# Late spread, late squares, a halved first weight unit and dummy matmuls in a two-layer streaming encoder step

## The reference

```python
for i in range(DEPTH):                       # 2 layers
    hp, hs = rms_norm(xp, mix_norm_g[i]), rms_norm(xs, mix_norm_g[i])
    if i % 2 == 0:                           # layer 0: spatial gating
        # z = gelu(h @ w_in); u, v = split(z); v = rms_norm(v)
        # y = u * (ws @ v in blocks of 128 positions + b);  m = y @ w_out
        mp, ms = sgu_mixer(hp, ...), sgu_mixer(hs, ...)
    else:                                    # layer 1: latent attention, 16 heads
        # a = h @ w_in; c_q, c_kv, k_r = split(a), each rms-normed (k_r rotated)
        # q = c_q @ w_uq; k, v = c_kv @ w_ukv; softmax(q k) v; @ w_o
        # the samples also see 1024 cached latents
        ...
    xp, xs = xp + mp, xs + ms
    xp = xp + square(relu(rms_norm(xp, g) @ w_up[i])) @ w_down[i]    # width 4096
    xs = xs + square(relu(rms_norm(xs, g) @ w_up[i])) @ w_down[i]
```

## Time and profile before

| | us |
|---|---|
| median of 3 runs | 1505.07 |
| lowest and highest | 1504.78, 1507.0 |
| the profiled execution | 1505.77 |
| its span, first to last instruction | 1504.0 |
| PE busy in it | 1474.6 |
| DVE, ACT, POOL busy | 799.6, 629.3, 765.8 |

### The profile page before, as it was taken

The page is one execution under the profiler, slowest core; times in us unless marked ns, Lnnn a source line. Parts: engine busy times, 40 slices in busy tenths (PEclk is TensorE's granted clock), DMA queues, the critical chain, the costliest instruction groups (busy, mean ns, idle before and its releaser), DMA issues.

```text
span 1504.0 us, 29170 instructions
## 1 busy us (share of the span) xinstructions
PE 1474.6 (98%) x10552; PEld 1384.2 (92%) x10552; DVE 799.6 (53%) x1417; ACT 629.3 (42%) x1248; POOL 765.8 (51%) x517
## 2 busy tenths in 40 slices
PE   9999999999999999999999999999999999999998
PEld 7789999999999999999996767686999999999998
DVE  6005716755654636537856464655446636456365
ACT  4413200123434434335447575767225435344342
POOL 7454455453463453644776464847433544535534
PEclk9999999999999999999999999999999999999999
DMA  7222242222232131331433010101121241412312
GB/s 233 86 82 82 60 121 72 68 84 62 66 115 82 60 122 42 121 102 57 142 112 97 2 57 1 56 0 56 43 71 58 84 127 43 139 56 84 112 56 91
DMA packets 36384, 120.32 MB, mean 80 GB/s; under 512 B 6040, under 2 KB 6744, under 8 KB 36064
## 3 DMA queue, kind: packets, MB, share of 16 engines
q1 hardware_dynamic: 30240, 109.20, 23.4%
q10 hardware_dynamic: 6080, 10.28, 2.2%
HBM read 115.91 MB, written 3.55 MB: 79 GB/s over the span
## 4 chain that ended last, share of the span: by engine, by line
PE 48%; ACT 2%; DVE 1%; issue 1%; ACTq 0%; DVEq 0%
PE ps L673 8%; PE ps L675 8%; PE ps L674 8%; PE ps L809 5%; PE ps L811 5%; PE ps L810 5%; PE ps L1065 2%; PE ps L905 2%; PE ps L1015 1%; PE ps L1029 1%; PE ps L910 1%; PE ps L1018 1%; ACT kT L1897 1%; PE ps L994 1%; DVE lat L1437 1%
## 5 line engine op out<-in xcount | busy, mean ns | idle before, releaser
L673 PE MATMUL ps<-h_hi,w_hi 128*128 128x288 f32 x1280 | 380.6, 297 | 0.0
L674 PE MATMUL ps<-h_lo,w_hi 128*128 128x288 f32 x1280 | 377.6, 295 | 0.0
L675 PE MATMUL ps<-h_hi,w_lo 128*128 128x288 f32 x1280 | 376.3, 294 | 0.0
L604 POOL TENSOR_TENSOR w_lo<-raw,w_hi 128x512 fp32r<-128x512 f32 x128 | 173.4, 1364 | 220.3 <-ACT w_hi L1725 220.0
L809 PE MATMUL ps<-op_hi,w_hi 128*128 128x288 f32 x896 | 266.3, 297 | 4.3 <-DVE x L1351 4.2
L810 PE MATMUL ps<-op_lo,w_hi 128*128 128x288 f32 x896 | 265.0, 296 | 0.0
L811 PE MATMUL ps<-op_hi,w_lo 128*128 128x288 f32 x896 | 264.2, 295 | 0.0
L675 PEld LDWEIGHTS ps<-h_hi,w_lo 128*128 128x128 f32 x1280 | 241.1, 188 | 0.0
L673 PEld LDWEIGHTS ps<-h_hi,w_hi 128*128 128x128 f32 x1280 | 239.8, 187 | 1.2
L674 PEld LDWEIGHTS ps<-h_lo,w_hi 128*128 128x128 f32 x1280 | 240.3, 188 | 0.0
L595 POOL TENSOR_TENSOR w_lo<-raw,w_hi 128x1024 fp32r<-128x1024 f32 x60 | 145.3, 2426 | 183.9 <-ACT w_hi L1717 183.9
(11 more groups left out here) (195 smaller groups left out, 2777.9 us busy)
## 6 DMA issues: line engine op xcount, KB each, us to landing
raw<-stream SPq DMA_DIRECT2D x206, 512.0 KB, 3.6
out_x<-x ACTq DMA_DIRECT2D x8, 288.0 KB, 2.5
x<-xt SPq DMA_DIRECT2D x4, 288.0 KB, 5.9
x<-xt ACTq DMA_DIRECT2D x4, 288.0 KB, 8.9
raw<-stream ACTq DMA_DIRECT2D x2, 512.0 KB, 6.9
b_bc<-bs ACTq DMA_DIRECT2D x2, 512.0 KB, 6.1
cache_raw<-cache_ct ACTq DMA_DIRECT2D x1, 1024.0 KB, 5.6
v_out<-sgu_grow ACTq DMA_DIRECT2D x1, 512.0 KB, 5.0
```

Source lines behind the costliest of these rows:

```text
L604: nc.gpsimd.tensor_tensor(block_of(w_lo, b), factor(i, b), block_of(w_hi, b).bitcast(F32), ALU.subtract).then_inc(split_lo, 1)
L673: nc.tensor.matmul(out, l_hi, r_hi, start=first, stop=False)
L674: nc.tensor.matmul(out, l_hi, r_lo, start=False, stop=False)
L675: return nc.tensor.matmul(out, l_lo, r_hi, start=False, stop=last)
```

## The change

It has five parts.

- **First unit.** POOL splits unit 0 in two halves of 512 columns, with a semaphore `first_half`; PE computes all five tiles with the first half, then with the second. The dummies at the start are 25 in place of 16.
- **First spread.** `norm_spread(0)` moves from chunk 0 to behind unit 2 of chunk 3, into banks 3 and 4, and waits there for ACT's reads of chunk 2. PE's wait for `rms_bc_set` moves behind chunk 3; ACT's `norm_take(0)` moves ahead of the reads of chunk 3. ACT loads the Gelu table early.
- **Order of reads.** In chunks 0 to 2 ACT reads tiles 3 and 4 first, then 0 to 2 (`v_place` gives a tile's place).
- **Late squares.** In the last quarter of the first MLP the squares of blocks 4, 5 and 6 go to three places of their own (`late_sq`, over `v_out`), and DVE adds them, and that of block 7, at the very end (`add_last_squares`). `norm_sums(2)` moves one unit later in chunk 4.
- **Dummies.** Two steps ("warm", n) in `attention_order`, each three dummy matmuls of `ident`, ahead of the transpose of key tile 11 and ahead of the sample scores.

```diff
-    steps = [("key", KT_N - 3), ("score", 0), ("score", 1), ("key", KT_N - 2), ("score", 2), ("key", KT_N - 1),
+    steps = [("key", KT_N - 3), ("score", 0), ("score", 1), ("warm", KT_N - 2), ("key", KT_N - 2), ("score", 2), ("key", KT_N - 1),
+             ("warm", KT_N - 1),
              ("samples", 0)]
...
+        late_sq = place("late_sq", [P, 3, T], F32, bump[0] - 4 * 512 - 4 * DS)
...
-        WARM, WARM_BANK = 16, 2
+        KEY_FILL = (3, 3)
+        WARM, WARM_BANK = 25, 2
...
+        def spread_banks(n):
+
+            return (3, 4) if n == 0 else (5, 6)
+
+        def v_place(t):
+
+            return t - 3 if t >= 3 else t + 2
...
-            for u in range(SLOTS):
+            left, right = slice(0, UNIT // 2), slice(UNIT // 2, UNIT)
+            pool.wait_ge(raw_loaded[0], 16)
+            nc.gpsimd.tensor_scalar(w_hi[:, 0, left], raw[:, 0, left], 1.0, 0.0, ALU.mult, ALU.add).then_inc(first_half, 1)
+            pool.wait_ge(first_half, 1)
+            nc.gpsimd.tensor_tensor(w_lo[:, 0, left], raw[:, 0, left], w_hi[:, 0, left].bitcast(F32),
+                                    ALU.subtract).then_inc(first_half, 1)
+            nc.gpsimd.tensor_scalar(w_hi[:, 0, right], raw[:, 0, right], 1.0, 0.0, ALU.mult, ALU.add).then_inc(split_hi, 1)
+            pool.wait_ge(split_hi, 1)
+            nc.gpsimd.tensor_tensor(w_lo[:, 0, right], raw[:, 0, right], w_hi[:, 0, right].bitcast(F32),
+                                    ALU.subtract).then_inc(split_lo, 1)
+            for u in range(1, SLOTS):
                 split(u, u, 0, first=True)
...
-                for j in range(4):
+                for j in range(1 if h_count == 0 else 0, 4):
...
-                            pe.wait_ge(tok_read, chunk * 5 + t + (1 if t < 3 else 6))
+                            if chunk < 4:
+                                pe.wait_ge(tok_read, 5 * chunk + v_place(t) + (1 if t < 3 else 6))
+                            else:
+                                pe.wait_ge(tok_read, chunk * 5 + t + (1 if t < 3 else 6))
...
+            pe.wait_ge(first_half, 2)
+            for k in range(2):
+                if k:
+                    pe.wait_ge(split_lo, 1)
+                pe.wait_ge(h_ready, k + 1)
+                w = slice(k * 512, k * 512 + 512)
+                for t in range(NT):
+                    last = three(ps[0:ROWS[t], bank_of(0, t), 0:512], h_hi[:, k, cols(t)], h_lo[:, k, cols(t)],
+                                 w_hi[:, 0, w], w_lo[:, 0, w], k == 0, False)
+            last.then_inc(unit_done, 1)
             token_chunk(0, 0, 0, 512, h_count=0,
-                        between={2: lambda: norm_sums(0), 3: lambda: norm_spread(0)})
+                        between={2: lambda: norm_sums(0)})
             pe.wait_ge(var_set, 2)
+            pe.wait_ge(pair_set, 2)
+
+            def spread_first():
+                pe.wait_ge(tok_read, 10 + 15)
+                norm_spread(0)
+
+            for c in range(1, 4):
+                token_chunk(c, c % 2, 4 * c, 512, pack=True, between={2: spread_first} if c == 3 else None)
             pe.wait_ge(rms_bc_set, 2)
-            pe.wait_ge(pair_set, 2)
-            for c in range(1, 4):
-                token_chunk(c, c % 2, 4 * c, 512, pack=True)
...
-            token_chunk(4, 0, L_IN, QL, between={1: lambda: norm_sums(2)}, h_count=2 * KD, tiles=F_O, halves_apart=True)
+            token_chunk(4, 0, L_IN, QL, between={2: lambda: norm_sums(2)}, h_count=2 * KD, tiles=F_O, halves_apart=True)
...
+                def warm(j):
+
+                    pe.wait_ge(vals_set, g * KT_N + (KT_N - 2))
+                    for _ in range(KEY_FILL[j - (KT_N - 2)]):
+                        nc.tensor.matmul(ps[:, key_bank(KT_N - 4), 0:P], ident[:], ident[:], start=True, stop=True)
...
+            def add_last_squares(s):
+
+                dve.wait_ge(x_sq, 8 * s)
+                for n, sq in enumerate((late_sq[:, 0, :], late_sq[:, 1, :], late_sq[:, 2, :], act_t[:, 1, :])):
+                    dve.wait_ge(sq_added, 9 * s - 7 + PAIRS + n)
+                    nc.vector.tensor_tensor(sq_sum[:], sq_sum[:], sq, ALU.add).then_inc(sq_added, 1)
...
-                            next_operand(i + 3, 1, next_s, 2 * i - 1)
+                            low_part(i + 3, next_s, 2 * i - 1)
...
-                        next_operand(7, 1, next_s, 7)
+                        low_part(7, next_s, 7)
+                        add_last_squares(next_s)
...
-            norm_take(0)
-
-
             act.wait_ge(rms_set, 1)
+            nc.scalar.activation(junk[:, 1:2], rms_tok[:, 0:1], ACT.Gelu)
             act.wait_ge(set_up, SETUPS)
             for c in range(4):
                 parity = c % 2
-                for t in range(NT):
+                if c == 3:
+                    norm_take(0)
+                for t in (range(NT) if c == 3 else (3, 4, 0, 1, 2)):
...
-                            operand_and_square(i + 4, 1, next_s)
+                            act.wait_ge(stored, 16)
+                            operand_and_square(i + 4, 1, next_s, i if i + 1 < PAIRS else None)
```

29 lines of the change are left out of this document (19 added, 10 removed).

## The result

The changed kernel took 1493.08 us (median of six runs, 1492.78 to 1493.48), the kernel before 1505.03 us beside it (1504.67 to 1507.0). The ratio of the runs, compared round by round, is 0.9915, 95% interval 0.9905 to 0.9925; on 1505.07 us, the median of before at the time of the forecast, that is 1492.3 us, a gain of 12.8 us (11.3 to 14.3). (The two medians alone give 0.9921 and 1493.1 us.) So it is faster, as forecast, and by more than forecast: trace against trace the gain is 12.3 us (span 1504.0 to 1491.7), where the sum had 10.7. The changed kernel's own median lies 0.3 us inside the lower end of the range, the time by the ratio 0.5 us under it.

A forecast was written before the change was run, and what follows sets the result against it. PE's own work was taken as the bound (busy 1474.6 of 1504.0 us), so only holes, passes and low clock pay. 2.2 + 2.7 + 2.8 + 3.0 = 10.7 us off 1505.77 gave 1495.1 us, range 1492.8 to 1499.2.

The forecast's parts named there:

- tail term: Put-off square adds on DVE before the statistics, after the first MLP: 0.5 us lost at the latents' transposes, bounds 0 and -4.8.
- Part A: Start: halved first unit and more dummies let PE begin 0.45 us sooner at full clock (1.73 us), 2.2 us gained.
- Rival 3: Start: dummies hold the first unit, PE begins up to 1.8 us later than summed, 1497 us, chance 0.05.
- Part B: First spread: waits of 2.25 and 1.73 us go, moved passes cost 1.25 us in chunk 3, 2.7 us gained.
- the bank wait: PE's wait at the next chunk's fourth tile for ACT to read its bank, 1.73 us, claimed to vanish.
- Part C: Last quarter of first MLP: put-off squares gain 1.7 us idle and 1.6 us low clock, less 0.5: 2.8 us.
- The hole: PE's 2.44 us idle before DVE's add into x, last quarter of first MLP: to shrink by 1.7 us.
- the low clock: Half-speed stretch of 3.3 us after that idle time in the first MLP's last quarter: 1.6 us gained by avoiding it.
- rival 2: Put-off square adds at 2.96 us each hold the statistics up: 1499.4 us, 1501 with a clock fall, chance 0.10.
- Part D: Head groups: dummies in holes before last key and sample scores keep full clock, 3.0 us gained, bounds 0 and 3.0.
- Rival 1: Clock still falls somewhere, each fall costing 1.25 to 1.75 us: 1496.4 to 1498.5 us, chance 0.24.
- Rivals 4 and 5: 4: ACT late at fourth tile, bank wait stays, 1496.8 us, chance 0.03; 5: DVE tail makes it slower, 1508.4 us, 0.02.

The follow-up runs named there:

- order_old: Changed kernel with ACT reading the tiles in the old order 0 to 4 in every chunk, late spread kept: 1493.03 us.
- undo_squares: Changed kernel with every square added in place again and the second norm's sums on PE one unit earlier: 1497.36 us.
- before_again: The kernel before, run again unchanged: 1505.69 us, 1.0005 of the kernel before beside it.
- before_moved: The kernel before plus nine one-column matmuls behind its 16 start dummies, nothing else: 1504.48 us, 0.9993 of the kernel before beside it.
- undo_start: Changed kernel with the first weight unit in one piece and 16 start dummies again: 1495.77 us.
- six_each: Changed kernel with six dummies in place of three at both places of each head group: 1494.32 us.

## Why the prediction was right or wrong

The direction and the mechanisms of all four parts were right, and the time by the ratio is 0.5 us under the range. The step that failed is the sum: it had no term for PE's third wait for x, near 515 us, which is worth 1.2 us, and its tail term of -0.5 us measured 0. The details follow.

**Part A: right, size right.** 2.2 us summed, 2.1 in the traces. (Undoing it cost 2.7 us, but that holds the hole near 512 us too: in the trace 2.3 for the start and 1.2 for the hole.) The first product came at 9.46 us (9.6 summed; 8.56 to 9.65 in other executions), without idle time, and the clock stayed up. Rival 3 (dummies hold the first unit) did not come true: the 50 passes took 8.24 us, 0.16 each. The next unit's low part was nearer to late than the argument had it, 0.4 us before PE wanted it and not 1.2. What the argument didn't see is that the clock was kept by a good margin: either half of the edit would have done.

**Part B: right.** 2.7 summed, 2.8 measured, 2.6 by undoing it. The copies went out of ACT's way and the passes came back in chunk 3. The order of reads, which the argument used for the bank wait, carries nothing (order_old).

**Part C: the mechanism right, the size too small.** 2.8 summed, 3.5 in the traces, 4.3 by undoing it. The hole (1.7 us) and the low clock (1.5, and 0.3 more in the blocks behind it) are as summed. The term that failed is the tail, -0.5 us: the latents' wait stayed at 0.76 us. DVE's three adds took 7.33 us, more than the 4.6 I took, and the statistic did come late: ACT has `rms_tok` at 751.97 us and starts the first latent straight behind it, at 752.21, where it sat idle for 4.11 us before. That is 0.9 us later relative to PE. Still PE's wait did not grow, since the delay is gone one step later, at DVE's `ss_lat`. DVE and POOL there, before:

```profile
766.64 2.02 DVE L1426 TENSOR_SCALAR ss_lat<-ss_lat 128x5 f32<-128x5 f32 x1 [10.09 <-ACT junk L1828]
766.24 2.40 POOL L582 TENSOR_TENSOR w_lo<-raw,w_hi 128x1024 fp32r<-128x1024 f32 x1
```

and after:

```profile
757.95 1.13 DVE L1486 TENSOR_SCALAR ss_lat<-ss_lat 128x5 f32<-128x5 f32 x1 [6.02 <-ACT junk L1891]
756.65 2.40 POOL L594 TENSOR_TENSOR w_lo<-raw,w_hi 128x1024 fp32r<-128x1024 f32 x1
```

DVE's instruction starts 0.9 us later relative to PE and is 0.9 us shorter. In both traces it ends with POOL's subtraction, at 768.66 and 759.08 us, and these are 9.6 us apart, as is all of PE's work there. So the subtraction, and not the statistic, ends last. How much more delay would have been hidden no run shows. I had read ACT's idle 4.11 us as all the slack there is, and the row of PE's wait as standing on that chain, which no row showed. undo_squares adds what the trace of before hid: a second hole of 1.3 to 1.9 us, which three of the four traces with the squares in place have (before_again, before_moved, undo_squares).

The Trainium skill (SBUF — State Buffer, "Who interferes with whom") says that such a DVE add and a GpSimd instruction block each other for a whole instruction. The rows agree: POOL works on weights without a pause from 733 to 743 us, three adds beside it take 7.33 us (2.44 each), and the fourth, begun in a pause of POOL, 0.76. By the rule rival 2's premise came nearly true (7.3 of 8.9 us). Of its conclusion half did: the statistics were held up, by 0.9 us, but not PE with them.

**Part D: right.** 3.0 summed, 3.0 in the traces over the groups (9.4 to 12.4 us of lead), 3.6 by undoing it, and the end of the bound was the right value. The dummies cost nothing, and all groups ran at full clock. Rival 1 (the clock falls somewhere all the same) had the largest chance of the rivals and didn't occur in any trace of the changed kernel or of the variants that kept all the parts.

**Missing: a term of 1.2 us.** The sum had no entry for the hole near 515 us. It was in the list of waits all along: 4.2 us in three waits for DVE's x, of which I named 2.44 and one of 0.9 and left the third without looking for its cause. Had I followed it (DVE, ACT, a weight unit, a code packet among its packets), I would still have had no way to know where the packet goes, but a gain of 1.2 us would have stood as an upper bound.

**The range.** 1492.8 us left out "a little below (if the tail costs nothing and the last holes close too)". The tail cost nothing (0.5), and the hole near 515 us closed (1.2). These two make 1.7 us, and the other terms cancel to -0.1, which gives the 1.6 us between 10.7 and 12.3. That alone gives 1493.5 us, which is what the profiled execution took, inside the range. The other 1.2 us down to 1492.3 are two things. I subtracted from the profiled 1505.77 us, and the time by the ratio counts from 1505.07: 0.7 us. And the ratio gives a gain of 12.8 us where the two traces give 12.3: 0.5 us, well within its interval. I had named the 0.7 us and kept the profiled base because I took it to hold a low stretch more than the others. That such stretches set the time of this kernel the record bears out (see before_again); whether the profiled execution had more than the two beside it, it doesn't show. With what is known now, the low end should have been near 1492.2 us: 1505.07 less 10.7, 1.2 for the third hole and 0.5 for the tail is 1492.7, and half a microsecond for the smaller holes. Rivals 4 and 5 did not occur.

## What to carry to other kernels

Undo a part on top of the whole change to learn its worth: in the trace of before one loss can hide the next, as the low clock hid PE's second hole, and the parts undone singly (2.7, 2.6, 4.3, 3.6 us) tell more than the first trace. Read their traces too, since an edit undone can bring back a loss elsewhere, as undo_start did. Filling short idle times with dummies is worth it for the clock even where the filled time itself gains nothing; what it costs to have a few too many can be read in one run (six_each, 1.2 us). And follow every wait in the list, the small ones too, down to the transfer that ends it, before a sum is called complete.
